# Query projection of cross attention: heads 1 to 3 as seven products of halves per pair of tiles, with one low part made by GpSimd

## The chip, the cores and the metric

The kernel runs on one core of one Trainium2 chip. The metric is the device time of one execution in microseconds (us), here the median of three runs: 1535.73 us (1535.05 to 1535.85). Everything is float32. The matmuls run on operands that are rounded to a "high" part, with a "low" part for the rest, so that one exact product takes three matmuls: high by high, high by low, low by high.

## The reference, cut to what matters

One inference step of an encoder layer on 1024 prompt tokens and 64 decode tokens (1088 in all), width 1024: a mixer, then cross attention with 4 heads of 256 features on 256 memory tokens, then a squared-ReLU MLP. The change is in the first line of the cross attention.

```python
def cross_attention(xn, mk, mv, w_xq, xq_norm, w_xo):
    q = rmsnorm((xn @ w_xq).reshape(bsz, t, N_HEADS_X, HEAD_DIM_X), xq_norm)
    s = jnp.einsum('bqhd,bkhd->bhqk', q, mk).astype(jnp.float32) * (HEAD_DIM_X ** -0.5)
    p = jax.nn.softmax(s, axis=-1).astype(mv.dtype)
    o = jnp.einsum('bhqk,bkhd->bqhd', p, mv).reshape(bsz, t, N_HEADS_X * HEAD_DIM_X)
    return o @ w_xo

yp = yp + cross_attention(rmsnorm(yp, norm_x[l]), mk, mv, w_xq[l], xq_norm[l], w_xo[l])
```

## The kernel before

Activations lie transposed: 8 tiles of 128 features by 1092 columns (1088 tokens and padding). `Y` holds the residual or the stage's result, `A` and `B` the high and low parts of a stage's operand. A dense stage makes output tiles one by one. Its weights come as slabs of 512 KB through `RAW` (two halves, loaded by SyncE), ScalarE makes the high part (`act_split`), VectorE the low part (`dve_split`), and TensorE does 8 x 3 x 3 matmuls of 364 columns (the last third has 360) for a tile (`pe_tile`, `pe_part`, line 424).

The stages around the change, in program order on TensorE: the output projection of the mixer, the query projection (8 tiles, slabs `S_XQ`, here 568.57 to 676.3 us of the trace), attention (20 units of scores, transposes and value products), its output projection (slabs `S_XO`), and the first layer of the MLP (slabs `S_UP`).

The query projection: `xq_tile(0)`, then a column sum of squares (`pe_stat`) of the whole residual; `act_root` and `dve_recip` turn it into the reciprocal norm, and two broadcasts (`pe_bcast`, line 477) placed between k blocks of tile 1 spread it over the partitions. ScalarE copies them into `RSTD`. `xevac` multiplies each finished tile by `RSTD` into `Y`. Two tiles are a head: ScalarE squares them (line 1304), `xq_stat` sums them, `dve_recip` inverts, two broadcasts spread, and `xq_nrm` (line 1935) scales the head in `Y`. `xscores(0)` to `xscores(2)` stand between the last k blocks of tile 7. SyncE loads the keys and values of heads 0 to 2 (`load_kv`, 4 transfers of 256 KB each) at the start of the stage.

The first layer of the MLP already has the form that the change brings: two tiles `up(0)`, `up(1)` in the plain way, while ScalarE and VectorE make combinations of the quarters of the input (`quad_scaled`, `t_raw` at line 2066, their high parts `t_hi` at line 1374, their low parts `t_lo` at line 2071), then 15 pairs of tiles by `product` (line 2836). A pair takes 7 products of halves in place of 8: 7 x 4 x 3 x 2 matmuls of 272 columns. For a pair, VectorE makes four combinations of the weights (`left_sum`, lines 2092 to 2100), ScalarE the high part of each product's weights (`left_hi`, line 1406), VectorE the low part (`left_lo`, line 2106), ScalarE copies three products out of PSUM (`prod_copy`, line 1388), and VectorE combines (`combine`, line 2122) and scales (`relu`, line 2135). There the pairs' weights alternate between two buffers, `RAW` and `RAWX`, and GpSimd makes quarter sums of the result (lines 961 to 974).

All order is written out by hand: each engine runs its own list, and semaphores with constant counts hold it up. The broadcasts on TensorE wait for the reciprocal:

```python
def norm_tile(i):
    tile_part(i, range(4))
    pe_bcast(e, cnt, 0, rc_wait(n_rc))
    tile_part(i, (4, 5))
    pe_bcast(e, cnt, 1)
    tile_part(i, (6, 7))
```

Tile 1 of the query projection does it after three k blocks and after the fourth.

## Time and profile before

| | |
|---|---|
| median of three runs | 1535.73 us (1535.05 to 1535.85) |
| span of the profiled execution | 1531.5 us, 26752 instructions |
| TensorE matmul busy | 1507.3 us (98%) |
| TensorE weight load busy | 1447.3 us (95%) |
| VectorE busy | 970.2 us (63%) |
| ScalarE busy | 592.3 us (39%) |
| GpSimd busy | 243.6 us (16%) |
| DMA, mean over the span | 124 GB/s |

The profile is one execution. Its span runs from the first to the last instruction; the time of that execution as a whole is not listed apart, and the median of the runs is 4.2 us above the span, which is what lies around it. Engines are named PE (TensorE matmul), PEld (TensorE weight load), DVE (VectorE), ACT (ScalarE), POOL (GpSimd) and SP (SyncE). A duration in a timeline row is from the start of the first to the shown end of the last instruction, and the next one starts some 0.1 us (on PE 0.2 to 0.3 us) before that shown end.

### The profile page before, as it was taken

To read this page: it belongs to the slowest core of one execution; us is meant where nothing else is said; L and a number is where in the kernel's file an instruction comes from. 1 tells how busy PE (TensorE), PEld (TensorE's weight loads), DVE (VectorE), ACT (ScalarE), POOL (GpSimd) and SP (SyncE) were. 2 spreads that over 40 slices of the span, in tenths; PEclk is the share of its full clock that TensorE was granted. 3 is DMA by queue.
4 is the path that set the end of the run, shared out by engine and by line. 5 is a ranking of instruction groups with operands and counts; after the bars stand their busy time and mean duration, and the time that the engine had idled before them with its cause. 6 is when DMAs were issued, how large, how long until landed. Compare 5 with 4: busy or idle time off the path is not lost.

```text
span 1531.5 us, 26752 instructions
## 1 busy us (share of the span) xinstructions
PE 1507.3 (98%) x10928; PEld 1447.3 (95%) x10928; DVE 970.2 (63%) x1370; ACT 592.3 (39%) x1021; POOL 243.6 (16%) x322
## 2 busy tenths in 40 slices
PE   8999999999999999998999999999999999999998
PEld 8999999997778999986899999999999999999998
DVE  7736777757777443457443896666665597547653
ACT  7521031146775221235322743333334344334332
POOL 1010000002100100000000054455444310010110
PEclk9999999999999999999999999999999999999999
DMA  8425111103102533022212244443344865354562
GB/s 279 142 98 176 54 42 42 45 1 103 68 29 71 163 127 136 15 73 71 85 73 85 85 158 158 150 151 128 133 177 177 325 230 181 117 178 121 185 213 100
DMA packets 64063, 189.33 MB, mean 124 GB/s; under 512 B 7888, under 2 KB 12040, under 8 KB 63808
## 3 DMA queue, kind: packets, MB, share of 16 engines
q1 hardware_dynamic: 39392, 95.30, 19.0%
q0 software_dynamic: 24560, 92.45, 16.8%
q8 instruction: 81, 1.33, 0.4%
q14 instruction: 30, 0.25, 0.1%
HBM read 138.58 MB, written 54.12 MB: 126 GB/s over the span
## 4 chain that ended last, share of the span: by engine, by line
PE 50%; DMA 4%; DVE 2%; issue 1%; ACT 1%; SPq 0%; DVEq 0%
PE ps L2836 20%; PE ps L2857 19%; PE ps L424 8%; DMA a<-wdn 3%; PE ps L2709 1%; PE ps L2676 1%; DVE B_lo L1985 0%; DMA r_raw_a<-quads_d 0%; DVE neg_max L1946 0%; PE ps L2687 0%; PE ps L2716 0%; DVE xpt_lo L1992 0%; ACT x_scores L1288 0%; ACT B_hi L1329 0%; DVE w_lo_b L411 0%
## 5 line engine op out<-in xcount | busy, mean ns | idle before, releaser
L424 PE MATMUL ps<-A_hi,w_hi 128*128 128x364 f32 (+1 forms) x768 | 171.2, 331 | 0.3 <-DVE Y L1554 0.3
L424 PE MATMUL ps<-A_lo,w_hi 128*128 128x364 f32 (+1 forms) x768 | 169.0, 328 | 0.0
L424 PE MATMUL ps<-A_hi,w_lo 128*128 128x364 f32 (+1 forms) x768 | 168.3, 327 | 0.0
L387 ACT ACTIVATE w_hi<-w_raw 128x1024 fp32r<-128x1024 f32 x42 | 44.2, 1058 | 286.2 <-PE ps L424 185.7
L424 PEld LDWEIGHTS ps<-A_hi,w_hi 128*128 128x128 f32 x768 | 130.8, 188 | 7.3 <-issue 6.6
L424 PEld LDWEIGHTS ps<-A_lo,w_hi 128*128 128x128 f32 x768 | 132.8, 188 | 0.0
L424 PEld LDWEIGHTS ps<-A_hi,w_lo 128*128 128x128 f32 x768 | 132.6, 188 | 0.0
L391 DVE TENSOR_TENSOR w_lo<-w_raw,w_hi 128x1024 fp32r<-128x1024 f32 x42 | 51.1, 1221 | 101.9 <-ACT w_hi L387 101.9
L2836 PE MATMUL ps<-t_hi,wq_hi 128*128 128x272 f32 x480 | 99.3, 288 | 0.3 <-issue 0.3
L2836 PE MATMUL ps<-t_lo,wq_hi 128*128 128x272 f32 x480 | 99.2, 288 | 0.0
L2836 PE MATMUL ps<-t_hi,wq_lo 128*128 128x272 f32 x480 | 99.1, 288 | 0.0
L2857 PE MATMUL ps<-r_hi_a,wq_hi 128*128 128x272 f32 x448 | 92.7, 288 | 1.7 <-DVE Y L2178 1.7
L2857 PE MATMUL ps<-r_lo_b,wq_hi 128*128 128x272 f32 x448 | 93.5, 290 | 0.0
L2857 PE MATMUL ps<-r_hi_b,wq_lo 128*128 128x272 f32 x448 | 93.3, 289 | 0.0
L2857 PE MATMUL ps<-r_hi_b,wq_hi 128*128 128x272 f32 x448 | 93.3, 289 | 0.0
L2857 PE MATMUL ps<-r_lo_a,wq_hi 128*128 128x272 f32 x448 | 92.7, 288 | 0.0
L2857 PE MATMUL ps<-r_hi_a,wq_lo 128*128 128x272 f32 x448 | 92.5, 287 | 0.0
L1614 DVE SCALAR_TENSOR_TENSOR conv_acc<-ua_ext,params,conv_acc 128x1118 f32<-128x1118 f32 x58 | 76.2, 1376 | 0.0
L2836 PEld LDWEIGHTS ps<-t_hi,wq_hi 128*128 128x128 f32 x480 | 75.2, 188 | 0.5 <-issue 0.5
L2836 PEld LDWEIGHTS ps<-t_lo,wq_hi 128*128 128x128 f32 x480 | 75.3, 188 | 0.0
L2836 PEld LDWEIGHTS ps<-t_hi,wq_lo 128*128 128x128 f32 x480 | 75.2, 188 | 0.0
L2836 PE MATMUL ps<-A_hi,wq_lo 128*128 128x272 f32 x360 | 74.5, 288 | 0.0
(327 smaller groups left out, 3570.4 us busy)
## 6 DMA issues: line engine op xcount, KB each, us to landing
w_raw<-slabs SPq DMA_DIRECT2D x67, 512.0 KB, 4.0
quads_d<-quad_sum POOLq DMA_DIRECT2D x64, 272.0 KB, 2.9
w_raw<-wdn POOLq DMA_DIRECT2D x32, 512.0 KB, 4.1
r_raw_a<-quads_d SPq DMA_DIRECT2D x56, 272.0 KB, 3.1
r_raw_b<-quads_d SPq DMA_DIRECT2D x56, 272.0 KB, 3.2
quads_d<-hid_stage POOLq DMA_DIRECT2D x48, 272.0 KB, 2.8
Y<-xT POOLq DMA_DIRECT2D x16, 546.0 KB, 4.8
y_d<-Y POOLq DMA_DIRECT2D x16, 546.0 KB, 3.2
```

The costliest lines, as they stand in the source:

```text
L387: e.activation(WH[:, par], RAW[:, par], ACT.Copy).then_inc(s.w_hi, 1)
L391: e.tensor_tensor(WL[:, par], RAW[:, par], WH[:, par].bitcast(F32), ALU.subtract).then_inc(s.w_lo, 1)
L424: ins = e.matmul(PS[:, 3 * par + c, 0:n_], wt[:, wpar, w], xt[:, col:col + n_], start=(first and n == 0 and m == 0), stop=(last and n == l ...
L1614: e.scalar_tensor_tensor(CAV[:, h], UE[:, h, j:j + CAW], w, CAV[:, h], ALU.mult, ALU.add)\
L2676: ins = e.matmul(PS[:, u % 3, b * NMEM:(b + 1) * NMEM], y(2 * h + k)[:, q0:q0 + P], XKV[h][:, kk, k * NMEM:(k + 1) * NMEM], start=(k == 0) ...
L2709: ins = e.matmul(PS[:, 6 + d, 0:w], wt[:, h, v0:v0 + P], xt[xturn(q)][:, k, 0:w], start=(m == 0 and k == 0), stop=(m == 2 and k == 1))
L2836: ins = e.matmul(PS[:, b + c, 0:HC], WQ[wx][:, n % 4, k * P:(k + 1) * P], right(i, xx, k, c), start=(i in (0, 1, 3) and k == 0 and m == 0) ...
L2857: ins = e.matmul(PS[:, 2 * g + c, 0:HC], WQ[wx][:, down_slot(n), g * P:(g + 1) * P], down_right(xx, n)[:, c * HC:(c + 1) * HC], start=(ii ...
```

## The change

Tiles 0 and 1 (head 0) stay as they are. Tiles 2 to 7 are made as three pairs (heads 1 to 3) by seven products each, `xproduct(0)` to `xproduct(20)`, in the manner of the MLP's first layer and with the same buffers for the combinations of the input. All pairs use the one buffer `RAW`: a half is reloaded when the combinations and low parts that read it are done. The low part of the last combination (`TL[3]`) is made by GpSimd, the others by VectorE. Since `Y` is both source of the combinations and target of the tiles, `xevac` of tiles 0 and 1 waits for all 16 instructions of `t_raw`. The keys and values, whose room the combinations take, are loaded once product 17, 19 and 21 is done (the count is of products, from 1). The squares of heads 0 to 2 go to `y(6)` and `y(7)`; their sums and broadcasts go to PSUM banks 0 or 6 in turn. `xscores(0)` to `xscores(2)` stand between the k blocks of the last product. The semaphores' counts in later stages are shifted by what the new stage adds, and the semaphore `ck_rc` is merged with `rm_rc`.

```diff
+N_XPAIR = 3
+N_XPROD = 7 * N_XPAIR
...
+        XSW = [at(f"xw_sum{k}", [P, 512], F32, A0 + (8 + k) * TB + 4 * HT) for k in range(4)]
+        XTMP = [at(f"xprod_tmp{k}", [P, HT], F32, A0 + k * TB + 4 * HT) for k in range(3)]
...
+        def stat_bank(h):
+
+            return 0 if h % 2 == 0 else 6
+
+        def xq_squares(h):
+
+            return [y(6), y(7)] if h < 3 else [XSQ[0][:, :], XSQ[1][:, :]]
...
+            for p in range(N_XPAIR):
+                for half in range(2):
+                    if p == 0:
+                        sp.wait_ge(s.w_lo, S_XQ + half + 1)
+                    elif half == 0:
+                        sp.wait_ge(s.sp_sum, 4 * p)
+                        sp.wait_ge(s.sp_lo, 7 * p - 3)
+                    else:
+                        sp.wait_ge(s.sp_lo, 7 * p)
+                    sp.dma_start(RAW[:, half], slabs[S_XQ + 2 + 2 * p + half]).then_inc(w_in[half], 16)
             sp.wait_ge(s.mem_stored, 32)
-            sp.wait_ge(s.tile_done, S_XQ)
             for h in range(3):
+                sp.wait_ge(s.prod, 17 + 2 * h)
                 load_kv(h)
-            with sp.Fori(S_XQ // 2 + 1, S_XO // 2) as i:
-                load(i, RAW)
-            sp.wait_ge(s.tile_done, S_XO)
+            sp.wait_ge(s.u_add, 3 * N_XPAIR)
+            load(S_XO // 2, RAW2, S_XO - C_XO)
...
+            for k in range(4):
+                g.wait_ge(s.t_hi, 12 + k + 1)
+                g.tensor_tensor(TL[3][:, k], TF[3][:, k], TH[3][:, k].bitcast(F32), ALU.subtract).then_inc(s.xt_lo3, 1)
...
+            def xleft_hi(n):
+
+                p, i = divmod(n, 7)
+                if n < 2:
+                    e.wait_ge(s.tile_done, S_XQ + 1)
+                elif n < 4:
+                    e.wait_ge(s.tile_done, S_XQ + 2)
+                else:
+                    e.wait_ge(s.prod, n - 3)
+                if i in (0, 3):
+                    xpair_wait(e, p, 0)
+                elif i == 6:
+                    xpair_wait(e, p, 1)
+                else:
+                    e.wait_ge(s.sp_sum, 4 * p + {1: 1, 2: 2, 4: 3, 5: 4}[i])
+                e.activation(WQ[0][:, n % 4], xleft(i), ACT.Copy).then_inc(s.sp_hi, 1)
...
+            def xsquares(h):
+                if h == 0:
+                    e.wait_ge(s.t_f, 16)
+                    e.wait_ge(s.y1_out, 128)
+                    e.wait_ge(s.tile_read, S_XQ + 2)
+                else:
+                    e.wait_ge(s.u_rel, 4 * h)
+                    e.wait_ge(s.stat_done, N_STAT_X + h)
+                if h == 3:
+                    e.wait_ge(s.prod, N_XPROD)
+                for k in range(2):
+                    e.activation(xq_squares(h)[k], y(2 * h + k), ACT.Square).then_inc(s.xs_sq, 1)
+
+            quad_scaled(1, "norm_x", S_OUT + 8)
+            t_hi(0, 0)
             act_root(e, cnt, D)
+            quad_scaled(3, "norm_x", S_OUT + 8)
+            xleft_hi(0)
+            t_hi(1, 0)
             act_bcast(e, cnt, RSTD)
+            t_hi(2, 0)
+            xleft_hi(1)
+            xleft_hi(2)
+            xprod_copy(0)
+            xsquares(0)
+            xleft_hi(3)
+            xprod_copy(1)
+            t_hi(3, 0)
+            xleft_hi(4)
+            xprod_copy(2)
+            xleft_hi(5)
+            act_root(e, cnt, 256, bank=stat_bank(0))
+            cnt.bc += 2
+            xleft_hi(6)
+            for n in range(7, N_XPROD):
+                p, i = divmod(n, 7)
+                xprod_copy(n - 4)
+                xleft_hi(n)
+                if i == 3:
+                    xsquares(p)
+                if i == 5:
+                    act_root(e, cnt, 256, bank=stat_bank(p))
+                    cnt.bc += 2
...
+            for u in range(3):
+                xexp(u)
+            xsquares(3)
...
+                e.wait_ge(s.t_x, 8)
+                e.wait_ge(s.t_f, 16)
...
+            t_raw(0, "norm_x", 0, 0)
+            t_raw(1, "norm_x", 0, 0)
+            t_lo(0, 0)
             dve_recip(e, cnt)
             cnt.bc += 2
+            t_raw(3, "norm_x", 0, 0)
+            xleft_lo(0)
+            t_raw(2, "norm_x", 0, 0)
             e.wait_ge(s.bc_used, cnt.used(cnt.bc))
-            for i in range(8):
-                if i < 6:
-                    dve_split(e, S_XQ + i + 2, i % 2)
-                if i == 7:
-                    xmin(0)
-                    xmin(1)
-                    xnorm(0)
-                    xmin(2)
-                    xnorm(1)
-                xevac(i)
-                if i % 2 == 0 and i:
+            xevac(0)
+            xevac(1)
+            xleft_sum(1)
+            xleft_sum(2)
+            xleft_lo(1)
+            t_lo(1, 0)
+            xleft_lo(2)
+            xleft_sum(4)
+            xleft_lo(3)
+            xleft_lo(4)
+            t_lo(2, 0)
+            xleft_sum(5)
+            xleft_lo(5)
+            xcombine(3)
+            dve_recip(e, cnt)
+            xleft_lo(6)
+            xcombine(4)
+            xq_nrm(0, 0)
+            xleft_lo(7)
+            xcombine(5)
+            xq_nrm(0, 1)
+            for n in (3, 4, 5):
+                xscale(n)
+            for n in (8, 9):
+                xleft_sum(n)
+                xleft_lo(n)
+            for n in range(10, N_XPROD):
+                p, i = divmod(n, 7)
+                xcombine(n - 4)
+                if n + 1 < N_XPROD:
+                    xleft_sum(n + 1)
+                xleft_lo(n)
+                xscale(n - 4)
+                if i == 5:
                     dve_recip(e, cnt)
-                    xq_nrm(i // 2 - 1, 0)
-                    xq_nrm(i // 2 - 1, 1)
+                if p == 2 and i < 2:
+                    xq_nrm(1, i)
+            xcombine(17)
+            xq_nrm(2, 0)
+            xscale(17)
+            xcombine(18)
+            xq_nrm(2, 1)
+            xscale(18)
+            xcombine(19)
+            xmin(0)
+            xscale(19)
+            xmin(1)
+            xnorm(0)
+            xmin(2)
+            xcombine(20)
+            xnorm(1)
...
+            def xproduct(n, ks=range(4)):
+
+                p, i = divmod(n, 7)
+                b = bank(p, i)
+                if ks[0] == 0:
+                    e.wait_ge(s.sp_lo, n + 1)
+                    if i == 0:
+                        e.wait_ge(s.bc_used, cnt.used(cnt.bc))
+                        e.wait_ge(s.stat_read, cnt.stat)
+                        if p == 1:
+                            e.wait_ge(s.tile_read, S_XQ + 1)
+                        elif p == 2:
+                            e.wait_ge(s.u_rel, 4)
+                    elif i == 1:
+                        if p == 0:
+                            e.wait_ge(s.tile_read, S_XQ + 2)
+                        else:
+                            e.wait_ge(s.u_add, 3 * p)
+                    elif i == 2:
+                        e.wait_ge(s.p_copy, 3 * p + 1)
+                    elif i == 3:
+                        if p == 0:
+                            e.wait_ge(s.tile_read, S_XQ + 2)
+                        else:
+                            e.wait_ge(s.u_add, 3 * p - 2)
+                    elif i == 4:
+                        e.wait_ge(s.p_copy, 3 * p + 3)
+                    elif i == 5:
+                        e.wait_ge(s.p_copy, 3 * p + 2)
+                    else:
+                        e.wait_ge(s.u_add, 3 * p + 2)
+                for k in ks:
+                    if p == 0 and i in (1, 2, 4):
+                        e.wait_ge(s.t_lo, 4 * {1: 0, 2: 1, 4: 2}[i] + k + 1)
+                    if p == 0 and i == 6:
+                        e.wait_ge(s.xt_lo3, k + 1)
+                    for m, (wx, xx) in enumerate(((0, 0), (0, 1), (1, 0))):
+                        for c in range(2):
+                            ins = e.matmul(PS[:, b + c, 0:HC], WQ[wx][:, n % 4, k * P:(k + 1) * P], right(i, xx, k, c),
+                                           start=(i in (0, 1, 3) and k == 0 and m == 0),
+                                           stop=(k == 3 and m == 2), skip_group_check=(i in (2, 4, 5, 6)))
+                if ks[-1] == 3:
+                    ins.then_inc(s.prod, 1)
...
+            for n in range(N_XPROD - 1):
+                p, i = divmod(n, 7)
+                xproduct(n)
+                if i == (2 if p == 0 else 1):
+                    if p == 1:
+                        e.wait_ge(s.u_rel, 4)
+                    xq_stat(p)
+                    n_rc += 1
+                if i == (4 if p == 0 else 3):
+                    pe_bcast(e, cnt, 0, rc_wait(n_rc), lo=stat_bank(p))
+                if i == (5 if p == 0 else 4):
+                    pe_bcast(e, cnt, 1, lo=stat_bank(p))
 
             def xscores(u):
 
                 h, p = divmod(u, 5)
                 kk = 0 if p < 4 else 2
-                e.wait_ge(s.bc_used, cnt.used(N_BC_X + 2 * h + (1, 1, 2, 2, 2)[p]))
+                e.wait_ge(s.bc_used, cnt.used(N_BC_X + (6 if u < 2 else 2 * h + (1, 1, 2, 2, 2)[p])))
+                if u == 2:
+                    e.wait_ge(s.u_add, 3 * N_XPAIR)
...
-            tile_part(7, range(4))
-            pe_bcast(e, cnt, 0, rc_wait(n_rc))
-            tile_part(7, (4,))
-            pe_bcast(e, cnt, 1)
-            e.wait_ge(s.tile_read, S_XO - 1)
             xscores(0)
-            tile_part(7, (5,))
+            xproduct(N_XPROD - 1, (0,))
             xscores(1)
-            tile_part(7, (6,))
+            xproduct(N_XPROD - 1, (1,))
             xscores(2)
-            tile_part(7, (7,))
+            xproduct(N_XPROD - 1, (2, 3))
```

## Rows read from the trace of the kernel before

**Rows 1.** The page: busy time of each engine.

```profile
PE 1507.3 (98%) x10928; PEld 1447.3 (95%) x10928; DVE 970.2 (63%) x1370; ACT 592.3 (39%) x1021; POOL 243.6 (16%) x322
```

**Rows 2.** The chain that ended last, in order of time (start us, us, what).

```profile
757.04 98.35 PE ps L424 x594
...
868.91 21.23 PE ps L2836 x168
...
890.40 283.37 PE ps L2836 x2256
```

**Rows 3.** Timeline of PE, query projection (start us, us, instruction, count, idle before).

```profile
585.76 0.42 PE L477 MATMUL ps<-stat_mix,row_sel 128*128 128x274 f32 x2
...
593.72 0.67 PE L424 MATMUL ps<-A_hi,w_hi 128*128 128x364 f32 x3
...
605.73 1.13 PE L465 MATMUL ps<-xq_sq,ones 128*32 128x273 f32 x16
```

**Rows 4.** Timeline of DVE, query projection.

```profile
568.99 1.30 DVE L1904 TENSOR_TENSOR Y<-ps,Y 128x1092 f32 x1 [4.34 <-PE ps L424]
...
613.36 1.48 DVE L1935 SCALAR_TENSOR_TENSOR Y<-Y,gq_scaled,ps 128x546 f32<-128x546 f32 x2 [1.16 <-PE ps L477]
```

**Rows 5.** Timeline of DVE at the start of the MLP's first layer.

```profile
843.73 1.29 DVE L1904 TENSOR_TENSOR Y<-ps,Y 128x1092 f32 x1 [4.34 <-PE ps L424]
...
859.25 1.86 DVE L510 RECIPROCAL stat_row<-stat_row 128x273 f32<-128x273 f32 x1
...
861.61 0.50 DVE L516 SCALAR_TENSOR_TENSOR stat_mix<-stat_row,row_mask,stat_mix 128x273 fp32r<-128x273 f32 x1
...
871.63 0.68 DVE L2092 TENSOR_TENSOR w_sum<-w_raw 128x512 f32<-128x512 f32 x1
...
873.07 0.69 DVE L2106 TENSOR_TENSOR wq_lo<-w_sum,wq_hi 128x512 fp32r<-128x512 f32 x1
873.68 2.62 DVE L2071 TENSOR_TENSOR t_lo<-t_raw,t_hi 128x544 fp32r<-128x544 f32 x4
```

**Rows 6.** Timeline of ACT, MLP's first layer.

```profile
872.94 0.60 ACT L1388 ACTIVATE prod_tmp<-ps 128x544 f32<-128x544 f32 x1
...
874.96 2.29 ACT L1374 ACTIVATE t_hi<-t_raw 128x544 fp32r<-128x544 f32 x4
```

**Rows 7.** Instructions of lines 961 (GpSimd) and 2100 (VectorE): duration ns min/median/max.

```profile
L961 POOL TENSOR_TENSOR quad_sum<-hid_stage x15: 1367/1870/1873, 897.3 to 1187.7; 128x544 f32<-128x544 f32 x15
...
L2100 DVE TENSOR_TENSOR w_sum<-w_raw,w_sum x8: 681/1840/1843, 876.8 to 1166.6; 128x512 f32<-128x512 f32 x8
```

**Rows 8.** DMA issues from 560 to 700 us: line, count, KB each, median us to landing.

```profile
w_raw<-slabs SPq DMA_DIRECT2D x6, 512.0 KB, 3.3
...
xkv<-mvc SPq DMA_DIRECT2D x4, 256.0 KB, 6.5
```

**Rows 9.** Timeline of ACT, end of the query projection.

```profile
676.48 2.29 ACT L1304 ACTIVATE xq_sq<-Y 128x1092 f32<-128x1092 f32 x2
```

**Rows 10.** Stretches: length, busy time and count of PE, PEld, DVE, ACT, POOL, then PEclk, DMA.

```profile
5.00:10.00 5.00, 2.33 (x11) 2.36 (x12) 2.80 (x7) 3.25 (x8) 0.71 (x1) 0.77 0.96 354
...
700.00:704.00 4.00, 2.29 (x14) 1.80 (x12) 3.82 (x8) 1.13 (x4) 0.53 (x1) 1.00 0.35 102
```

**Rows 11.** Timeline of PE, first 15 us.

```profile
7.67 0.52 PE L2255 MATMUL ps<-mem_hi,w_hi 128*128 128x256 f32 x1 [2.84 <-DVE mem_lo L1492]
...
10.12 0.41 PE L2255 MATMUL ps<-mem_hi,w_lo 128*128 128x256 f32 x1
10.34 0.41 PE L2255 MATMUL ps<-mem_hi,w_hi 128*128 128x256 f32 x1
...
12.25 0.28 PE L2255 MATMUL ps<-mem_lo,w_hi 128*128 128x256 f32 x1
12.37 0.28 PE L2255 MATMUL ps<-mem_hi,w_lo 128*128 128x256 f32 x1
```

359 lines of the change are left out of this document (200 added, 159 removed).

## The prediction

> **What bounds the kernel now.** I read the busy times first: the matmuls fill 1507.3 of 1531.5 us and the engine beside them at most 63% [rows 1]. The chain that ended last runs on TensorE through all the dense stages, without a gap in long pieces [rows 2]. So the time is TensorE's work plus its gaps, and a change pays what it takes off TensorE less the gaps that it opens. Next I read the timelines of the query projection and of the start of the MLP's first layer, where the same form is in use already: they show where TensorE will ask for something and when the other engines have it.
>
> **What a pair saves.** 594 matmuls of 364 columns took 98.35 us, 165.6 ns each; 2256 of 272 columns took 283.37 us, 125.6 ns each, and the first 168 took 21.23 us, 126.4 ns [rows 2]. Two tiles were 144 x 165.6 ns = 23.8 us; seven products are 168 x 125.6 ns = 21.1 us. Three pairs save 3 x 2.7 = 8.2 us, on the path. The rest of the edit has to be hidden behind 3.0 us products, and I went through the lists of all engines in order. For that the price of a step is its distance to the next row: 0.60 us for a VectorE operation of 512 columns and 0.65 of 544 (four of these 2.62) [rows 5], 0.52 for ScalarE's high part or copy, 2.2 for four of `t_hi` [rows 6], 1.1 us a square [rows 9], and 0.1 to 0.2 us from one engine to another. Durations of rows 5 and 6 stand for the new lines, which have the same shapes.
>
> **First gap: the first broadcast, 1.7 us.** Before, the first broadcast came at 585.76 with no wait [rows 3]. Now VectorE does `t_raw(0)`, `t_raw(1)`, `t_lo(0)` ahead of the reciprocal, as it does in the MLP's layer. That layer's timeline is this one's, 274.74 us later (843.73 against 568.99 for the last residual tile, [rows 4, 5]). There the reciprocal ran from 859.25 and its last step ended at 862.11 [rows 5], which is 587.37 here. The MLP's layer has four k blocks ahead of the broadcast; this stage has three, so TensorE is there at 585.7 and waits until 587.4. It can't be less unless VectorE's list is quicker than the same list was there. Product 0 then starts at 595.4 in place of 593.72 [rows 3].
>
> **Second gap: product 1, 0.5 us.** It needs the sum `a21+a22`, which stands behind `xevac(0)` and `xevac(1)`, and the second of these waits for the end of tile 1. From 595.4: 0.2 to VectorE, 1.2 for the second evacuation, then from the start of the sum to the end of its low part 2.1 us (871.63 to 873.76, [rows 5]), in all 599.0; product 0 is done at 598.4. In the MLP's layer the second product is one that needs no sum, so that this doesn't show there.
>
> **Third gap: the broadcast behind product 4, 4.4 us.** It waits for head 0's reciprocal, and VectorE has that behind a long chain. Product 1 ends at 602.1; ScalarE copies it (0.7 with the hand-over), makes four `t_hi(3)` (2.2), then the high part for product 4 (0.6): 605.6. VectorE: its low part 0.6, four of `t_lo(2)` 2.6, the sum for product 5 0.6, over to ScalarE and back 0.8, low part 0.6, combination of product 3 0.65, reciprocal with its two mixing steps 2.85 [rows 5]: 614.4. To that comes GpSimd: its four subtractions start as soon as `t_hi(3)` is there, in the middle of this. When GpSimd works on two SBUF operands, VectorE's operation on two SBUF operands shows 1.84 in place of 0.68 us [rows 7], 1.16 more for each GpSimd one. The first falls in VectorE's wait, the second partly, and two stand between the `t_lo(2)`: 0.1 + 2 x 1.16 = 2.4 us. So the reciprocal is there at 616.8. TensorE has product 2, head 0's sums (1.1, [rows 3]), products 3 and 4, and is done at 602.1 + 9.1 + 1.1 = 612.3. It stands 4.4 us. Without the collision it would be 2.0. GpSimd's own result is no bound: it is wanted by product 6.
>
> The Trainium skill (page "SBUF — State Buffer", section "SBUF: two separate sides") says that the port pair that VectorE and GpSimd share is an exclusive lock, held for a whole instruction, and that the loser blocks. Read with GpSimd's shown 1.87 us [rows 7] as the hold, the sum below would come out some 2.5 us higher; the trace's 1.84 us operation speaks for a shorter hold.
>
> **Fourth gap: head 1's sums behind product 8, 1.7 us.** From the end of product 5 VectorE has: combination 0.65, head 0's second scaling 1.4 (two in 1.48, [rows 4]), three `xscale` 1.9, sum, high part and low part for product 8 2.0, the same for product 9 2.0, combination of product 6 0.65; then ScalarE squares twice, 2.1; with the hand-overs 11.1 us. TensorE has a broadcast and products 6, 7, 8, 9.4 us.
>
> **Fifth gap: the second broadcast of head 1, 2.6 us.** The last pair's second half of weights is loaded into the one buffer once the low part of product 13 is made. From the end of product 9: copy and high part 1.2, low part 0.7, the load 3.3 us to landing [rows 8] and 0.1, sum 0.6, low part of product 14 0.6, `xscale` 0.65, first half of head 1's scaling 1.5: 8.9 us. TensorE has two products and one broadcast, 6.3. The load is bound by 3.3 us from below and by the 6.5 of the keys' and values' transfers [rows 8] from above; I take 3.3, since nothing else is in flight then.
>
> **The last two heads and attention, 0.6 us.** By the same count the third pair has VectorE's work ready in time, head 2's broadcasts too. The keys and values of head 0 are asked for after product 16; 1.4 us of issue and 6.5 us to landing [rows 8] make 7.9, the scores come after three products and two broadcasts, 9.6 us later. Head 1's and 2's come earlier than wanted as well. Before, ScalarE ended the last squares 2.3 us after the last matmul of tile 7 (676.3 to 678.6, [rows 9]), because the first of them was done before; now both wait for product 20, 3.1 us, and its cover between the scores is thinner. I take 0.6 for this (0 to 1). ScalarE's and VectorE's attention work behind is the same as before.
>
> **The sum.** Gaps 1.7 + 0.5 + 4.4 + 1.7 + 2.6 = 10.9, five restarts of TensorE at 0.1 = 0.5, attention 0.6: 12.0. Less 8.2: +3.8 us on the span, 1531.5 to 1535.3. What lies around the span is 4.2 us and doesn't change, so 1535.7 + 3.8 = 1539.5 us. The stages behind are untouched but for shifted counts.
>
> **The rivals.** *The ports don't collide, or less.* If VectorE passes GpSimd's four subtractions, the third gap is 2.0 and the sum is +1.4: 1537.1 us. For it: the combinations that read PSUM show no such delay. Against it: `t_lo(2)` reads two SBUF operands like line 2100. A fourth gap that closes since the third gave VectorE time would give about the same, 1537.8.
>
> *TensorE's clock falls in the third gap.* At the start it stood 2.84 us [rows 11] and the granted clock of the stretch is 0.77 [rows 10]: matmuls stood 0.22 us apart at 10.1 and 0.12 at 12.3 [rows 11]; over the 3.3 us from 7.67 to some 11 us that is 15 of them at 0.1 us more, 1.5 us. In the stretch from 700 to 704 it was busy for 2.29 of 4 us and kept 1.00 [rows 10]. A gap of 4.4 us is longer than either. If it costs 1.5, the time is 1541.0. The Trainium skill (page "TensorE: Matmul & The Clock Gate", section "HAM oscillation — how this bites in real kernels") says that idle gaps let the engine fall to its lower clock and every such gap is paid anew; no row here shows it after the start. A GpSimd hold longer than 1.16 us, or a slower load, ends there too: 1541 to 1543.
>
> *The other side: the work beside TensorE hides.* In the MLP's layer it does: from 868.91 the seven products ran with 0.26 us idle behind them, up to 890.40 [rows 2]. If the lists here had the same slack after the first gap, it would be 8.2 - 1.7 - 0.1 - 0.6 = 5.8 us less: 1529.9 us. It decides in the third gap: the reciprocal would have to be ready 12 us after the start of product 1, where I count 17.7. That layer has two weight buffers and no head norm in between, which is what speaks against this.
>
> *It doesn't do what it says.* The counts of products and shapes are in the diff; only the rate of 272-column matmuls could differ, and 126.4 ns at the start of that layer bounds this at 0.4 us.
>
> **How the numbers follow.** The forecast, with its five gaps within a microsecond in all, 0.50: 1538.5 to 1540.5, mostly above the bound of 0.2% (3.1 us, about what a measurement of this kernel can tell from no change), so 0.40 slower and 0.10 same. Less collision or a closed gap, 0.24: same. Clock or longer holds, 0.18: slower. All hidden, 0.08: faster, 0.07 by more than 0.2%. In sum slower 0.58, same 0.35, faster 0.07. The range goes from 1536.3, a microsecond under the first rival, to 1543.0, the clock and a hold of GpSimd's full time together, and leaves out the 0.08 and some tails.
>
> **What would show it.** In the profile after: an idle of 1.7 us at the first broadcast near 587, released by the mixing step; TensorE idle of 4 us near 612 to 617, at a broadcast, released by VectorE's mixing step; VectorE's low parts beside GpSimd's four at 1.8 us; 1.7 us ahead of the sums of head 1 released by ScalarE's squares; 2.6 us at a broadcast near 643 with VectorE waiting for `w_raw` just before. The attention stage should be as long as before within 1 us. The prediction is wrong if the third gap is under 2 us, if the order of VectorE's list lets the reciprocal pass, or if a transfer of the keys comes late and opens a sixth gap at the first scores.

## The result, and the profile after

The changed kernel took 1541.31 us (median of 7 runs, 1539.37 to 1544.48), the kernel before 1535.47 us beside it (7 runs, 1532.66 to 1537.58). The ratio is 1.0043, interval 1.0033 to 1.0052: slower by 0.43%. The forecast was 1539.5 us, slower, range 1536.3 to 1543.0. The profiled span is 1539.5 us in place of 1531.5, its mean granted clock 0.996 in place of 0.998.

Busy times of the profile after, which answer to [rows 1]: TensorE is shown busy for 1.3 us less, and not for the 8.2 us that the pairs leave out, in a span that is 8.0 us longer. The slow matmuls that follow below are 4.4 us of the difference.

```profile
PE 1506.0 (98%) x11000; PEld 1444.1 (94%) x11000; DVE 1012.2 (66%) x1440; ACT 618.0 (40%) x1069; POOL 250.9 (16%) x326
```

TensorE's timeline after, the rows of the query projection that begin behind an idle of 0.2 us or more (in brackets its length and what released it), and one row that follows:

```profile
586.65 0.52 PE L485 MATMUL ps<-stat_mix,row_sel 128*128 128x274 f32 x2 [1.51 <-DVE stat_mix L524]
...
598.30 0.52 PE L2885 MATMUL ps<-t_hi,wq_hi 128*128 128x272 f32 x2 [0.42 <-DVE wq_lo L2118]
...
616.49 0.82 PE L485 MATMUL ps<-stat_mix,row_sel 128*128 128x274 f32 x2 [4.22 <-DVE stat_mix L524]
617.11 0.66 PE L2885 MATMUL ps<-A_hi,wq_hi 128*128 128x272 f32 x2
...
632.33 1.13 PE L473 MATMUL ps<-Y,ones 128*32 128x273 f32 x16 [1.60 <-issue]
...
645.36 0.52 PE L485 MATMUL ps<-stat_mix,row_sel 128*128 128x274 f32 x2 [2.43 <-DVE Y L2047]
```

These are five gaps, where the forecast had them, and no sixth one. Their sum is 10.2 us. In the projection before there was none of 0.2 us or more.

The chain that ended last, after (start, length, what; the last two answer to [rows 2]):

```profile
617.32 3.98 PE ps L2885 x24
...
645.88 13.58 PE ps L2885 x96
...
666.98 3.00 PE ps L2885 x24
...
698.31 3.03 PE ps L2966 x12
...
710.66 4.59 PE ps L2966 x12
...
764.07 98.35 PE ps L432 x594
...
875.92 21.27 PE ps L3077 x168
```

Two pairs of pieces are to be compared here: 24 matmuls of one product take 3.00 us at 666.98 and 3.98 behind the third gap; 12 of the attention's value products take 3.03 us at 698.31 and 4.59 at 710.66. TensorE waits for nothing inside these pieces. The granted clock shows why (stretches of 4 us; the last three columns are clock, DMA share, GB/s):

```profile
612.00:616.00 4.00, 0.27 (x3) 0.05 (x1) 3.53 (x5) 1.82 (x4) 0.00 (x0) 0.99 0.37 131
616.00:620.00 4.00, 3.51 (x18) 3.51 (x19) 3.65 (x6) 0.00 (x0) 0.00 (x0) 0.58 0.37 131
620.00:624.00 4.00, 4.00 (x34) 4.00 (x33) 2.67 (x5) 0.00 (x0) 0.00 (x0) 1.00 0.00 0
```

TensorE stood for almost all of 612 to 616, came back at a clock of 0.58 on average, near its lower level of 1.2 GHz, and had 2.4 GHz again in the next window.

VectorE and GpSimd ahead of the third gap:

```profile
606.01 4.96 DVE L2095 TENSOR_TENSOR t_lo<-t_raw,t_hi 128x544 fp32r<-128x544 f32 x4
...
602.86 6.25 POOL L986 TENSOR_TENSOR t_lo<-t_raw,t_hi 128x544 fp32r<-128x544 f32 x4 [32.53 <-ACT t_hi L1345]
```

Four low parts that took 2.62 us in [rows 5] take 4.96 us beside GpSimd's four.

### The profile page after: what moved, and what is told of

It is laid out like the page before. It is cut to its first block, busy times and chain, and to the rows that moved or that the text cites. A ratio compares the mean times of both kernels' runs of the same rounds, so it can differ in the third digit from the quotient of the medians.

```text
span 1539.5 us, 27052 instructions
## 1 busy us (share of the span) xinstructions
PE 1506.0 (98%) x11000; PEld 1444.1 (94%) x11000; DVE 1012.2 (66%) x1440; ACT 618.0 (40%) x1069; POOL 250.9 (16%) x326
## 3 DMA queue, kind: packets, MB, share of 16 engines
q8 instruction: 81, 1.33, 0.3%
## 4 chain that ended last, share of the span: by engine, by line
PE 60%; DVE 4%; DMA 4%; ACT 2%; issue 1%; SPq 0%; DVEq 0%; ACTq 0%
PE ps L3077 20%; PE ps L3098 19%; PE ps L432 14%; DMA a<-wdn 3%; PE ps L2885 3%; PE ps L2966 1%; PE ps L2931 1%; DVE t_lo L2095 1%; DVE B_lo L2215 0%; DMA r_raw_a<-quads_d 0%; DVE t_raw L2090 0%; ACT scores L1235 0%; PE ps L473 0%; PE ps L485 0%; PE ps L2753 0%
## 5 line engine op out<-in xcount | busy, mean ns | idle before, releaser
L432 PE MATMUL ps<-A_hi,w_hi 128*128 128x364 f32 (+1 forms) x624 | 138.7, 330 | 0.3 <-DVE Y L1661 0.3
L432 PE MATMUL ps<-A_lo,w_hi 128*128 128x364 f32 (+1 forms) x624 | 137.3, 328 | 0.0
L432 PE MATMUL ps<-A_hi,w_lo 128*128 128x364 f32 (+1 forms) x624 | 136.7, 327 | 0.0
L395 ACT ACTIVATE w_hi<-w_raw 128x1024 fp32r<-128x1024 f32 x36 | 37.9, 1059 | 242.7 <-PE ps L432 142.4
L432 PEld LDWEIGHTS ps<-A_hi,w_hi 128*128 128x128 f32 x624 | 106.1, 188 | 5.8 <-issue 5.3
L432 PEld LDWEIGHTS ps<-A_lo,w_hi 128*128 128x128 f32 x624 | 107.9, 188 | 0.0
L432 PEld LDWEIGHTS ps<-A_hi,w_lo 128*128 128x128 f32 x624 | 107.7, 188 | 0.0
L399 DVE TENSOR_TENSOR w_lo<-w_raw,w_hi 128x1024 fp32r<-128x1024 f32 x36 | 43.8, 1221 | 69.8 <-ACT w_hi L395 69.8
```

What stands on the lines that cost most here:

```text
L395: e.activation(WH[:, par], RAW[:, par], ACT.Copy).then_inc(s.w_hi, 1)
L399: e.tensor_tensor(WL[:, par], RAW[:, par], WH[:, par].bitcast(F32), ALU.subtract).then_inc(s.w_lo, 1)
L432: ins = e.matmul(PS[:, 3 * par + c, 0:n_], wt[:, wpar, w], xt[:, col:col + n_], start=(first and n == 0 and m == 0), stop=(last and n == l ...
```

## The experiments

Two lengths are read from each profile: from the first matmul of the projection to the first of the scores (the projection), and to the first matmul of attention's output projection (projection and attention). They leave out the other stages, which together differ by up to 3 us between these fourteen profiles. Between the kernel before and a changed one only the second length is fair: at the first scores the kernel before still has three k blocks of 1.5 us to do, a changed one four of 0.75 us, which makes the first length of before 1.5 us shorter. Gaps are named 1 to 5 as above. What a gap costs in clock is read as the distance from the delayed broadcast to the next one, less the 3.35 us that this has at full speed (617.11 to 620.46 with the fillers below), or as a piece of the chain less the same piece elsewhere. Each kernel has one profile; a length in the table is of that execution alone. The kernels were timed in four series, in which the kernel before had a median of 1535.47 (changed), 1535.07 (the next four), 1535.88 (the four after them) and 1536.39 us (the last four), so that ratios compare better than medians. The ratios are those of the record, with 95% intervals; they are not the quotients of the medians.

```
kernel                     gaps 1 to 5 (us)              projection  + attention  median us (ratio, interval)
before                     none                             97.91      175.49     1535.1 to 1536.4
changed                    1.51 0.42 4.22 1.60 2.43        105.30      183.30     1541.31 (1.0043, 1.0033-1.0052)
fillers in gaps 3, 5       1.51 0.42 0.42 1.60 0.59        102.97      180.81     1537.97 (1.0019, 1.0007-1.0030)
GpSimd late                1.52 0.42 2.73 1.61 2.37        103.57      181.57     1539.57 (1.0027, 1.0015-1.0040)
first reciprocal first     -    1.33 4.20 1.61 2.35        103.36      181.39     1541.47 (1.0044, 1.0027-1.0061)
two orders (gaps 4, 5)     1.52 0.42 4.23 1.26 -           102.16      180.19     1537.41 (1.0018, 1.0009-1.0028)
head 0's reciprocal early  1.51 0.42 2.43* 1.60 2.44       100.40      178.36     1538.05 (1.0013, 1.0004-1.0022)
all orders                 -    1.34 2.45* 1.25 -           98.29      176.28     1533.40 (0.9985, 0.9976-0.9994)
VectorE for GpSimd         1.51 0.42 1.76 1.59 2.29        101.66      179.36     1539.43 (1.0027, 1.0013-1.0041)
before, one gap            4.32 (made)                     104.80      184.04     1540.74 (1.0033, 1.0021-1.0046)
all orders, VectorE        -    1.35 1.03* 1.71+ 1.25 -     97.49      175.37     1533.36 (0.9979, 0.9968-0.9989)
all orders, GpSimd late    -    1.32 1.04* 0.49+ 1.26 -     95.96      173.96     1532.59 (0.9965, 0.9951-0.9979)
 the same, filler          the same                         95.96      172.37     1529.72 (0.9952, 0.9938-0.9965)
before, filler             none                             97.90      175.40     1534.95 (0.9995, 0.9984-1.0006)
* the wait is product 4's   + a new wait, at the second broadcast of head 0 or at product 7
```

**Fillers in the gaps.** 30 matmuls on old data ahead of the broadcast behind product 4, 18 ahead of head 1's second broadcast; the result is thrown away.

```diff
+                if p == 0 and i == 4:
+                    fill(30, 1)
                 if i == (4 if p == 0 else 3):
                     pe_bcast(e, cnt, 0, rc_wait(n_rc), lo=stat_bank(p))
+                if p == 1 and i == 4:
+                    e.wait_ge(s.u_add, 4)
+                    fill(18, 5)
```

> The changed kernel with filler matmuls of 272 columns (30 ahead of the broadcast behind product 4, 18 ahead of the second broadcast of head 1; their results are read by nobody) so that TensorE works where it stood idle for 4.2 and 2.4 us. Nothing else moves. Theory 'gaps and clock': the waits end at the same times, but products 5 and 12, which took 4.0 and 4.5 us behind the gaps, take 3.0 again, the broadcast too: 2.8 us less than the changed kernel, and a granted clock of 1.00 from 616 to 650. The 2.8 us gap in attention is left alone and may still lose 1.5. Rival 'the products behind the gaps are long for another reason (operands, PSUM banks)': they stay at 4.0 and 4.5 us and the time stays.

TensorE's timeline with fillers:

```profile
612.73 3.96 PE L2907 MATMUL ps<-A_hi 128*128 128x272 f32 x30
...
617.11 0.52 PE L485 MATMUL ps<-stat_mix,row_sel 128*128 128x274 f32 x2 [0.42 <-DVE stat_mix L524]
```

The broadcast came no earlier, the wait is the same. But the granted clock stayed 1.00 up to the end of the projection, and the projection got 2.3 us shorter, the median 3.3 us. The ten timed runs bear it out: their mean granted clock is 0.998, that of the changed kernel's seven runs 0.9954, and the two ratios' intervals don't meet. So matmuls that compute nothing, in a gap that stays as long, pay. The low clock is an effect of the idle, and it is a cost of its own. For gap 3 one profile is enough, since every unfilled gap of 4.2 us in the table was followed by it; for gap 5 it isn't, since in three other kernels such a gap cost nothing (see the last section).

**GpSimd late.** GpSimd waits until the low part of left factor 5 is made.

```diff
+            g.wait_ge(s.sp_lo, 6)
             for k in range(4):
                 g.wait_ge(s.t_hi, 12 + k + 1)
```

> The changed kernel with GpSimd's four subtractions held back until the low part of product 5 is made, so that they run beside the reciprocal. Theory 'port': the four operations of t_lo(2) take 2.6 in place of 4.96 us, the low part of product 4 0.7 in place of 1.1, and the gap at the broadcast behind product 4 falls from 4.2 to 1.7 us, by 2.5; with it the clock drop behind that gap may go, 1.2 more. In all 2.5 to 3.7 us less. Rival 'the chain is as long without GpSimd': t_lo(2) stays near 5 us, the gap at 4.2, no change in time.

VectorE with GpSimd late:

```profile
611.49 1.86 DVE L518 RECIPROCAL stat_row<-stat_row 128x273 f32<-128x273 f32 x1
613.45 0.38 DVE L522 TENSOR_SCALAR stat_mix<-stat_row,row_mask 128x273 fp32r<-128x273 f32 x1
613.87 1.45 DVE L524 SCALAR_TENSOR_TENSOR stat_mix<-stat_row,row_mask,stat_mix 128x273 fp32r<-128x273 f32 x1
615.24 1.82 DVE L2119 TENSOR_TENSOR wq_lo<-w_raw,wq_hi 128x512 fp32r<-128x512 f32 x1
```

The low part of T2 took 2.62 us again, and gap 3 fell to 2.73, not to the 1.7 us that was expected. The collision had only moved: the mixing step that the broadcast waits for shows 1.45 in place of 0.50 us, the low part behind it 1.82 in place of 0.68. The reciprocal and the step at 613.45, which have one SBUF operand of full width, show no such delay beside the same GpSimd work. In the median this run can't be told from the changed kernel (the intervals overlap, 1.0015 to 1.0040 and 1.0033 to 1.0052); the profile's stage is 1.7 us shorter.

**VectorE for GpSimd.** VectorE makes these four low parts, behind the low part of factor 6; GpSimd has nothing to do.

```diff
-            for k in range(4):
-                g.wait_ge(s.t_hi, 12 + k + 1)
-                g.tensor_tensor(TL[3][:, k], TF[3][:, k], TH[3][:, k].bitcast(F32), ALU.subtract).then_inc(s.xt_lo3, 1)
...
             xleft_lo(6)
+            for k in range(4):
+                e.wait_ge(s.t_hi, 12 + k + 1)
+                e.tensor_tensor(TL[3][:, k], TF[3][:, k], TH[3][:, k].bitcast(F32), ALU.subtract).then_inc(s.xt_lo3, 1)
```

> Undoes one part of the change: VectorE, and not GpSimd, makes the low part of the last row combination, behind the low part of left factor 6; GpSimd has nothing to do there. Theory (the two engines share a port, each GpSimd instruction holds VectorE up by 1.1 us): the low part of T2 takes 2.6 us again in place of 4.96, the gap behind product 4 falls from 4.2 to 1.9 us; VectorE has 2.6 us more behind it, the normalisation of head 0 comes later by that, and product 6 follows without a wait; the total is 1 to 2.5 us below the changed kernel: 1539 to 1540 us. Rival (no collision, the low part of T2 waited for something else): the gap stays at 4.2 us and the total is the same or up to 2.6 us more.

VectorE and TensorE in this kernel:

```profile
605.93 2.62 DVE L2091 TENSOR_TENSOR t_lo<-t_raw,t_hi 128x544 fp32r<-128x544 f32 x4
...
614.07 0.52 PE L485 MATMUL ps<-stat_mix,row_sel 128*128 128x274 f32 x2 [1.76 <-DVE stat_mix L524]
```

Gap 3 fell from 4.22 to 1.76 us: 2.46 us of it were the collision (forecast 2.4). VectorE's 2.6 us more opened no wait above 0.3 us. Even so the clock fell behind the 1.76 us, at 614.72, for 1.5 us of loss (0.45 us from pair to pair up to 617.89). The projection got 3.6 us shorter in the profile, the median 1.9, with intervals that still touch (1.0013 to 1.0041 and 1.0033 to 1.0052). In this place, the part of the change that relieves VectorE cost more than it relieved.

**First reciprocal first.** The reciprocal of the input norm goes ahead of the low part of T0.

```diff
-            t_lo(0, 0)
             dve_recip(e, cnt)
             cnt.bc += 2
+            t_lo(0, 0)
```

> The changed kernel with VectorE's reciprocal of the residual's norm ahead of t_lo(0) in its list. Theory 'list order': the first broadcast waits for nothing (gap of 1.5 us gone), and everything behind it, the other gaps among them, keeps its length, so 1.5 us less. Rival 'VectorE is the bound of the stage': the 1.5 us come back in the gap behind product 4 (5.7 in place of 4.2), no change in time.

Gap 1 is gone, gap 2 grew from 0.42 to 1.33: TensorE got there 1.5 us earlier, the sum for product 1 only 0.6. A net of 0.6 us, where 1.5 were expected; the other 1.3 us of the shorter projection fit the clock, which did not fall behind gap 5 this time (its 1.5 us are missing). The median doesn't show it (1541.47 us, four runs).

**Two orders.** The combination of product 6 ahead of the sum for product 9, and head 1's first scalings ahead of the third pair's sums, which wait for the load.

```diff
                 xleft_lo(n)
+                if n == 8:
+                    xcombine(6)
...
-                xcombine(n - 4)
+                if n > 10:
+                    xcombine(n - 4)
+                if p == 2 and i < 2:
+                    xq_nrm(1, i)
                 if n + 1 < N_XPROD:
```

> The changed kernel with two moves in VectorE's list: the combination of product 6 ahead of the sum and low part for product 9, and the scalings of head 1 ahead of the weight sums of the third pair. Theory 'list order': the gap ahead of head 1's sums falls from 1.6 to 0.3 us or less, the gap at head 1's second broadcast from 2.4 to 0, and with it the clock drop in product 12 (1.5 us): 5.0 us less in all. Rival 'the load into the one weight buffer is the bound': the 2.4 us gap moves to product 14 or 15, and only 1.3 us are won.

Gap 5 went; gap 4 only fell from 1.60 to 1.26, where 0.3 or less was expected. What is left is ScalarE's order. In its timeline (with the VectorE row that makes what is squared in front) the squares, which end when TensorE's wait ends, stand behind two high parts, and the first of these waits for a sum of VectorE:

```profile
629.35 0.72 DVE L2137 TENSOR_TENSOR Y<-ps,rstd 128x544 f32<-128x544 f32 x1
...
630.76 0.63 ACT L1362 ACTIVATE wq_hi<-xw_sum 128x512 fp32r<-128x512 f32 x1 [2.05 <-DVE xw_sum L2109]
...
631.82 2.11 ACT L1385 ACTIVATE Y<-Y 128x1092 f32<-128x1092 f32 x2
```

What the squares read is there at 630.1, and they start at 631.82. Squares ahead of those high parts is an order that no run here tried. The slow stretch behind gap 3 was longer than in the changed kernel with the same gap (timeline of TensorE; 0.45 us from one pair to the next in place of 0.25):

```profile
617.14 0.83 PE L485 MATMUL ps<-stat_mix,row_sel 128*128 128x274 f32 x2 [4.23 <-DVE stat_mix L524]
617.76 0.66 PE L2888 MATMUL ps<-A_hi,wq_hi 128*128 128x272 f32 x2
...
622.29 0.66 PE L2888 MATMUL ps<-A_lo,wq_hi 128*128 128x272 f32 x2
```

From this broadcast to the next it is 6.02 us (4.64 in the changed kernel): 2.7 us lost against 1.3, behind the same gap.

**Head 0's reciprocal early.** ScalarE's root ahead of the high part of factor 5; on VectorE the reciprocal ahead of the low part of T2.

```diff
-            xleft_hi(5)
             act_root(e, cnt, 256, bank=stat_bank(0))
             cnt.bc += 2
+            xleft_hi(5)
...
-            t_lo(2, 0)
             xleft_sum(5)
+            dve_recip(e, cnt)
+            t_lo(2, 0)
             xleft_lo(5)
             xcombine(3)
-            dve_recip(e, cnt)
```

> Moves the root of head 0's statistics on ScalarE ahead of the high part of left factor 5, and on VectorE the reciprocal ahead of the low part of T2 (four instructions that the GpSimd work stretches to 4.96 us together) and of the low part of left factor 5. Theory of the order (the gap of 4.2 us behind product 4 is VectorE's queue, and the clock falls because of the gap): the gap goes to 0.5 us or less, the low clock behind it goes with it, product 5 waits up to 1 us for the low parts that are now later; the broadcast ends about 3 us earlier and the projection is 4 to 5 us shorter: 1536.5 to 1537.5 us. Rival 1 (the reciprocal waits for the statistics' column sums and ScalarE, not for the queue): the gap stays above 2.5 us. Rival 2 (the time that the GpSimd work takes from VectorE only moves): the gap is taken over by a wait of product 5 for the low part of T2 or of factor 5, of 3 us or more, and the total stays within 1 us of the changed kernel.

The wait moved ahead of product 4, and became 2.43 us. The first rival falls, the second is partly right: of 4.22 us 1.8 went, and the rest changed its place. The clock stayed at its upper level in the whole projection of this profile, which with the 1.8 us gives most of the 4.9 us that it is shorter; the median is 1538.05, above the 1536.5 to 1537.5 us that were expected.

**One gap in the kernel before.** Eight multiplications on VectorE ahead of head 1's reciprocal.

```diff
                 if i % 2 == 0 and i:
+                    if i == 4:
+                        e.wait_ge(s.stat_read, cnt.stat + 1)
+                        for k in range(8):
+                            e.tensor_tensor(TH[k // 4][:, k % 4], RSTD[:, 0:HT], RSTD[:, HT:2 * HT], ALU.mult)
                     dve_recip(e, cnt)
```

> The kernel before, with eight multiplications of 128x544 put on VectorE (0.60 us apart in a row, 4.9 us together) ahead of one reciprocal of the X projection, that of head 1: nothing else is changed, and no product is left out. It prices one gap of TensorE alone. The broadcast has about 1.2 us of slack, so TensorE should stand for 3.5 to 4 us in front of it. Theory of the clock (TensorE comes back at a lower granted clock after a gap of that length): some 3 to 5 us of matmuls behind the gap take up to twice as long, a loss of 1.2 to 1.5 us on top of the gap, so +4.9 to +5.3 us in all: 1540 us. Rival (the low clock of the changed kernel has to do with its products and not with a gap): +3.5 to +4 us, matmuls behind the gap at the same spacing of 0.165 us.

TensorE's timeline around the made gap:

```profile
637.95 0.66 PE L424 MATMUL ps<-A_hi,w_lo 128*128 128x364 f32 x3
642.93 0.83 PE L477 MATMUL ps<-stat_mix,row_sel 128*128 128x274 f32 x2 [4.32 <-DVE stat_mix L516]
643.55 1.11 PE L424 MATMUL ps<-A_hi,w_hi 128*128 128x364 f32 x3
...
647.18 1.10 PE L424 MATMUL ps<-A_lo,w_hi 128*128 128x364 f32 x3
...
649.38 0.65 PE L424 MATMUL ps<-A_lo,w_hi 128*128 128x364 f32 x3
```

Three matmuls of 364 columns show 1.11 us behind the gap and 0.65 later; from 643.55 to 648.09 five such groups took 4.54 us in place of 2.49, 2.05 lost, and the two broadcasting matmuls 0.62 in place of 0.36. The gap of 4.32 us cost the projection 6.9 us (97.91 to 104.80). None of the changed products is in this kernel. So this gap cost its length and half as much again, without any part of the change. It settles the rival that the slow matmuls come from the changed products.

**All orders.** The last three diffs on the changed kernel together (first reciprocal, two orders, head 0's reciprocal).

> All orders together: reciprocal of the projection's norm ahead of the low part of T0, reciprocal of head 0's statistics and its root early, the sixth product's combination ahead of the sum of factor 9, head 1's scaling ahead of the third pair's sums. Theory (the loss of the change is waits behind VectorE's queue, and the low clock behind them): of the gaps of 1.5, 0.4, 4.2, 1.6 and 2.4 us there stay 0, 1.3, 0.5, 1.3 and 0, sum 3 in place of 10.2, and the low clock in the projection (2.7 us) goes; 7 + 2.7 = 10 us less than the changed kernel: 1530 to 1532 us, some 4 us faster than before. Rival (the work of the three products more that the halves leave out is not saved in full, or the waits come back elsewhere): 1534 us or more. Rival of the clock (the low clock comes from the lighter load of the attention that follows, not from the gaps): the same gaps, but 1533 us.

It is faster than the kernel before, by 0.15% (0.06 to 0.24), at 1533.40 us in place of the expected 1530 to 1532. The gaps are 5.0 us in place of 10.2, where 3 were expected: product 4 waits for 2.45 us. The clock still fell once, behind product 4's wait (timeline of TensorE):

```profile
611.01 0.49 PE L2888 MATMUL ps<-t_hi,wq_hi 128*128 128x272 f32 x2 [2.45 <-DVE t_lo L2095]
...
614.70 0.58 PE L2888 MATMUL ps<-t_hi,wq_hi 128*128 128x272 f32 x2
615.12 0.41 PE L2888 MATMUL ps<-t_lo,wq_hi 128*128 128x272 f32 x2
```

In the profile of "head 0's reciprocal early" the same wait is 2.43 us, and the clock kept 1.00 behind it. Behind head 1's second broadcast, where gap 5 is gone, its four products take 12.06 us in place of 13.58:

```profile
640.58 12.06 PE ps L2888 x96
```

**All orders, with VectorE or with GpSimd late.** The first is all orders and the diff of "VectorE for GpSimd"; the second is all orders and one wait, for the low part of T2:

```diff
+            g.wait_ge(s.t_lo, 12)
             for k in range(4):
                 g.wait_ge(s.t_hi, 12 + k + 1)
```

> The orders of the run with all orders, and VectorE makes the low part of the last row combination (behind the low part of left factor 6) in place of GpSimd. In the run with all orders product 4 waited 2.45 us for the low part of T2, which took 4.96 us beside the GpSimd work. Theory (port): that part takes 2.6 us, the wait of product 4 goes to 0.1 to 0.3 us, the low clock behind it (1.5 us lost) goes too, VectorE's 2.6 us more are hidden: 3.5 to 4 us less than with all orders, 1529.5 to 1530 us, 0.4% faster than before. Rival (VectorE is too full for it): a new wait at product 6 or at head 1's column sums of 1.5 us or more, 1532 us or more.

> The same orders, with the work left on GpSimd, which starts it only when VectorE has made the low part of T2. Theory: the wait of product 4 goes as in the run with VectorE; GpSimd's four instructions now fall on the low parts of factors 5 and 6 and on the first combinations, which have slack; the same time within 1 us: 1529.5 to 1530.5 us. Rival (the collision finds another instruction on the path): a wait of 1 us or more at product 5 or 6, 1531 us or more.

One sentence of the first expectation is a misreading: with all orders the low part of T2 took 2.62 us, since GpSimd was through by then; what GpSimd held up was the low part of factor 4 and the sum of factor 5, ahead of the reciprocal. In both kernels product 4's wait is 1.0 us and not 0.3, and the clock kept 1.00 in the projection. With VectorE a wait of 1.71 us came in front of head 0's second broadcast, behind the 2.6 us more that VectorE has to do; with GpSimd late there are 0.49 us ahead of product 7 instead, and the projection is 1.5 us shorter in the profile. Here GpSimd's help pays in the stage, where it doesn't run beside VectorE's steps on the path; the medians (1533.36 and 1532.59 us, eight and five runs) don't tell the two apart. Both medians are 2 to 4 us above what I expected.

**A filler in attention.** 20 matmuls into a free bank, in the gap of 2.8 us that the attention of both kernels has. Once on the best kernel so far, once on the kernel before.

```diff
+                if q == 3:
+                    e.wait_ge(s.x_pt, 7)
+                    e.wait_ge(s.x_plo, xlows(7))
+                    for _ in range(20):
+                        e.matmul(PS[:, 3, 0:HC], XV[0][:, 0, 0:P], XV[0][:, 0, 0:HC], start=True, stop=True)
                 e.wait_ge(s.x_pt, 5 * h + (2, 4, 5)[g])
```

> The run before this (orders, GpSimd late), with 20 matmuls of 272 columns into a free bank in the attention's gap of 2.81 us behind the scores of unit 11; their result is thrown away. Nothing gets shorter but that gap, which they fill to 0.4 us. In every profile of a kernel with a changed projection the value products behind this gap ran 1.3 to 1.5 us longer than in the profile before. Theory (the clock falls because of the gap): they take 3.0 us again, 1.3 us less than without the fillers: 1528.5 to 1529 us. Rival (the clock there has another cause, the light attention as a whole): the value products are as slow as without.

> The kernel before with the same 20 matmuls in the same gap of its attention. Its one profile showed no low clock behind the gap. If that is so in its timed runs too, the fillers change nothing (within 0.3 us of before); if the one profile was a lucky one, 1 to 1.5 us less than before, a ratio of 0.999.

TensorE's timeline in that attention, first the changed kernel, then the best kernel with the filler:

```profile
710.66 0.71 PE L2966 MATMUL ps<-xpt_hi,xv_hi 128*128 128x512 f32 x2 [2.81 <-issue]
711.21 0.80 PE L2966 MATMUL ps<-xpt_lo,xv_hi 128*128 128x512 f32 x2
711.81 1.05 PE L2966 MATMUL ps<-xpt_hi,xv_lo 128*128 128x512 f32 x2
```

```profile
700.60 2.75 PE L2959 MATMUL ps<-xv_hi 128*128 128x272 f32 x20
703.65 0.70 PE L2975 MATMUL ps<-xpt_hi,xv_hi 128*128 128x512 f32 x2 [0.30 <-issue]
704.20 0.63 PE L2975 MATMUL ps<-xpt_lo,xv_hi 128*128 128x512 f32 x2
```

With the filler the value products are as quick as elsewhere and attention is 1.6 us shorter. The median is 1529.72 us, 0.48% faster than before (0.35 to 0.62). It is 2.9 us below the run without the filler, but with five runs each and intervals that overlap, the 1.6 us of the profile are the better figure. On the kernel before, the same filler gave 1534.95 against 1536.39 us, with an interval that holds no change as well as 1.5 us; its stages were as long as before's (175.40 and 175.49), since the one profile of before has no low clock there.

## Why the prediction was right, and where it fell short

**What a pair saves: right.** The products behave as in [rows 2]: 3.00 us for 24 matmuls, 21.27 us for the 168 of the MLP's start. That the 8.2 us are there shows best with the gaps small: in "all orders, GpSimd late" the gaps are 4.1 us and the clock keeps 1.00, -8.2 + 4.1 is -4.1, the projection to the first value product was 3.4 us shorter than before. 0.7 us are left for restarts and what lies between; I had 0.5.

**The five gaps: right one by one.** 1.51, 0.42, 4.22, 1.60 and 2.43 us against 1.7, 0.5, 4.4, 1.7 and 2.6; the sum 10.2 against 10.9. (The steps listed for the fifth gap add up to 8.65 us and not to 8.9, which gives 2.35.) The reasons are seen too. Gap 1 is the order of VectorE's list (it goes with the first reciprocal first). Gap 2 is the sum for product 1 behind the evacuations. Gap 3 is 1.8 of VectorE's list and 2.4 of the collision. Gap 4 has VectorE and then ScalarE in it, 0.35 of it from VectorE's order. Gap 5 is the load and the scaling behind it: VectorE's timeline has the wait that was forecast,

```profile
641.98 0.69 DVE L2106 TENSOR_TENSOR xw_sum<-w_raw 128x512 f32<-128x512 f32 x1 [1.55 <-DMA w_raw<-slabs]
```

and the gap goes when the scaling is put ahead of that wait.

**The collision: right in size.** VectorE steps on two full SBUF operands took up to 1.2 us longer beside GpSimd's subtractions, as in [rows 7]: 4.96 for 2.62 us is two of them. Others took only 0.4 to 0.5 us longer (1.13 for 0.69 us for the low part at 604.96 in the changed kernel, 1.22 and 1.15 us for two low parts in "all orders, GpSimd late"); the forecast had 0.1 for the first of these. GpSimd's four took 5.49 us in the GpSimd-late run, 1.37 each. The forecast weighed a rule of a lock for the whole instruction (the Trainium skill, page "SBUF — State Buffer", section "SBUF: two separate sides") with GpSimd's shown 1.87 us as the hold, and that was too long: gap 3 came at 4.22 us. With 1.37 us as the hold the same rule gives, as an estimate, 2.7 us for two of them where 2.3 were measured, so that these runs don't speak against it. (Two holds of 1.87 in place of 1.16 us would add 1.4 us; the forecast's 2.5 doesn't follow from its terms.)

**Attention: 0.6 us forecast, 1.9 measured** (62.13 us from the first value product to the output projection in place of 60.22, with 0.4 of it in a longer wait for the last squares, 0.60 in place of 0.16). The rest is the clock, 1.6 us behind the 2.81 us gap.

**The clock: the step that was mis-sized.** It stood outside the sum, as a rival that costs 1.5 us once, in the third gap, with longer holds in the same chance of 0.18. In the profile it came behind all three gaps above 2.4 us: behind gap 3 1.3 us (4.64 us from broadcast to broadcast in place of 3.35); behind gap 5 1.5 us (13.58 against 12.06 for the same 96 matmuls); behind the attention's 2.81 us 1.6 (4.59 against 3.03). That is 4.4 us. In the profiles the account to the end of attention is -8.2 + 10.2 of gaps + 4.4 of clock + 0.4 of attention's wait + 1.0 left for restarts and what lies between = +7.8, which is what they show (183.30 against 175.49). The forecast had +3.8.

What misled me was [rows 10]: I took the attention's gap of 2.80 us in the profile before, with the clock at 1.00, as a length that is safe. The stretch that I showed, 700 to 704 us, can't even tell this, since it ends inside the gap. The rows behind it (timeline of TensorE, kernel before) do show full speed, 0.47 to 0.54 us from pair to pair:

```profile
705.09 0.70 PE L2709 MATMUL ps<-xpt_hi,xv_hi 128*128 128x512 f32 x2 [2.80 <-issue]
705.63 0.62 PE L2709 MATMUL ps<-xpt_lo,xv_hi 128*128 128x512 f32 x2
706.10 0.62 PE L2709 MATMUL ps<-xpt_hi,xv_lo 128*128 128x512 f32 x2
```

But all eleven other profiles that have this gap without a filler, the kernel before with one made gap among them, paid 1.3 to 1.6 us there. The one profile of before was the exception. The right reading would have been: one instance bounds nothing from above, and the start of the kernel ([rows 10, 11], 0.77 behind 2.84 us) was the other instance. The Trainium skill (page "TensorE: Matmul & The Clock Gate", section "HAM oscillation — how this bites in real kernels") tells of a kernel that pays anew behind every idle. These runs agree in part: each idle can cost 1.3 to 2.7 us anew, but the clock did not fall behind each of them, as the last section shows.

**The median and the profile differ, and the clock is most of it.** The median rose by 5.8 us and the profiled spans by 8.0. In every run on record some 1.8 us lie around the span (1541.31 and 1539.5), not the 4.2 us of the section on the profile before. That figure cancels in the forecast, but it hid that the profiled execution of before was a quick one: some 1533.3 us (an estimate, 1531.5 + 1.8), 2.2 below the median of its seven runs. Over the 65 runs of before that were timed beside the experiments, time goes with the mean granted clock: 1534.4 us on average for the 24 runs at 0.999, 1536.2 for the 24 at 0.998, 1538.2 for the 8 at 0.995 or 0.996, which is about 1.1 us for 0.001. Before has 0.998 on average, the changed kernel's seven runs 0.9954, and so, as an estimate, 2.8 us more of clock. With the gaps, the attention's wait and the rest as in the profile this is -8.2 + 10.2 + 2.8 + 0.4 + 1.0 = +6.2, near the 5.8 of the medians. In other words, the timed runs of before seem to pay part of the attention's clock too. The filler on the kernel before points that way (0.9995 of before, 0.8 us, at a clock of 0.9988 against 0.9981) and doesn't settle it.

So the forecast of 1539.5 us lies 1.8 us below the median because the clock was not in its sum; the other terms were together 0.4 us too high (12.0 of gaps, restarts and attention, 11.6 found). Its range, 1536.3 to 1543.0 us, had room for the clock.

**The other side** (the work hides, 1529.9 us) did not come by itself, but it shows what was there: with the order of the lists changed and the idle in attention filled, the same products gave 1529.72 us. That the two numbers nearly meet is chance: this kernel still has 4.1 us of gaps in the projection, and a filler in attention that the forecast did not have. In the profile of the changed kernel the order of the lists and the shared port (10.2 us of gaps) and the clock behind the waits (4.4 us, 1.6 of them behind a gap that before has too) took 14.6 us from the 8.2 that the pairs saved.

## What to carry to other kernels

An edit that takes matmuls away pays only as far as the other engines' lists fit the shorter time: walk the list of each in order, and put what TensorE waits for (reciprocals, scalings) ahead of what is only due later. Count an idle of TensorE at its length and, from some 2.7 us on, at 1.3 to 2.7 us more: that came in 16 of 17 cases in the projection and attention of these kernels, and for 2.3 to 2.45 us in three of seven. Where an idle can't be closed, matmuls on old data in it save this second part. Work given to GpSimd should run where VectorE's steps are off the path.

## What was not expected of the hardware

- How much a gap costs in clock changes from one to the next of the same length: 4.2 to 4.3 us of idle lost 1.3, 1.5, 2.7 and 2.3 us; 2.8 us in attention lost 1.3 to 1.6 eleven times and nothing once; 2.73 us lost 1.4 once; 2.3 to 2.45 us lost 1.5 three times and nothing four times; 1.76 us lost 1.5 once. Gaps of 1.0 to 1.7 us in the projection were never followed by a low clock. What decides within these is open.
- The fall can come late: in the changed kernel TensorE came back at 645.36 at full speed and slowed down only at 646.47, with no idle in between:

```profile
646.47 0.50 PE L2885 MATMUL ps<-A_hi,wq_hi 128*128 128x272 f32 x2
646.77 0.65 PE L2885 MATMUL ps<-A_lo,wq_hi 128*128 128x272 f32 x2
```

- A VectorE reciprocal, or a step with one full SBUF operand, ran beside GpSimd's subtractions at its usual length (1.86 and 0.38 us), while steps with two such operands grew by 0.95 to 1.14 us in the same run (0.4 to 1.2 us in all runs).
